# Linear attention outputs scaled head by head by ScalarE and turned by the identity; the third unit's first scores ahead of the first turns

## The reference, cut to what matters

```python
def gla_output(o, r, gain):
    B, T = o.shape[:2]
    o = o * lax.rsqrt(jnp.mean(o * o, axis=-1, keepdims=True) + EPS) * gain.astype(jnp.float32)
    return (o.reshape(B, T, GLA_V_W) * jax.nn.silu(r.astype(jnp.float32))).astype(r.dtype)
```

```python
def win_attend(qg, q_pos, k, v, k_pos, slopes):
    dist = (q_pos[:, None] - k_pos[None, :]).astype(jnp.float32)
    mask = (k_pos[None, :] >= 0) & (dist >= 0) & (dist <= WINDOW)
    s = jnp.einsum('bhgtd,bshd->bhgts', qg, k).astype(jnp.float32) * (NSA_HEAD_DIM ** -0.5) - slopes[None, :, :, None, None] * dist
    p = masked_softmax(s, mask)
    return jnp.einsum('bhgts,bshd->bhgtd', p.astype(v.dtype), v)
```

## Time and profile before

| | |
|---|---|
| median of 3 runs | 1752.52 us (1752.28 to 1753.33) |
| profiled execution, its own time | 1760.71 us |
| its span in the trace | 1758.9 us |
| TensorE matmuls busy | 1684.2 us, 96% of the span |
| VectorE busy | 1093.2 us, 62% |
| GpSimd busy | 830.2 us, 47% |
| ScalarE busy | 518.2 us, 29% |
| mean granted clock of TensorE | 0.978 of 2.4 GHz |
| linear attention stage | from 321.1 to 389.8 us of the span |
| sparse attention stage | from 390.0 us |

### The profile page before, as it was taken

One profiled execution on the slowest core, in us unless ns is written; L12 is line 12 of the kernel. 1 busy time (PEld: TensorE's weight loads), 2 busy tenths in 40 slices (PEclk: granted clock), 3 DMA queues, 4 the chain that ended last, 5 costly groups with the idle time before them and its releaser, 6 DMA issues.

```text
span 1758.9 us, 24643 instructions
## 1 busy us (share of the span) xinstructions
PE 1684.2 (96%) x9310; PEld 1369.3 (78%) x9310; DVE 1093.2 (62%) x2113; ACT 518.2 (29%) x1100; POOL 830.2 (47%) x644
## 2 busy tenths in 40 slices
PE   8999999897999989999999989999999999999997
PEld 7888888784555557777778878888888888888886
DVE  5332111446776667776641068896789678967897
ACT  3311111337887762334222162100120012001202
POOL 3211221314454452413222189957685668476933
PEclk9999999988999999999999999999999999999999
DMA  5488893838434545646643541121021201211005
GB/s 154 138 256 255 237 278 93 247 98 268 158 126 126 175 132 216 252 161 231 223 154 108 173 170 59 50 71 59 14 72 48 72 7 66 69 52 46 3 1 193
DMA packets 172396, 233.53 MB, mean 133 GB/s; under 512 B 22488, under 2 KB 137096, under 8 KB 168120
## 3 DMA queue, kind: packets, MB, share of 16 engines
q1 hardware_dynamic: 162024, 181.64, 33.6%
q0 software_dynamic: 9216, 50.34, 8.0%
q10 hardware_dynamic: 1040, 0.00, 0.0%
HBM read 217.58 MB, written 102.45 MB: 182 GB/s over the span
## 4 chain that ended last, share of the span: by engine, by line
PE 65%; DVE 6%; issue 2%; ACT 2%; POOL 2%; another core or an unknown queue 0%; DVEq 0%
PE PS L3137 36%; PE PS L2217 7%; PE PS L2415 6%; PE PS L1870 4%; PE PS L1855 4%; PE PS L1883 4%; DVE Z L2597 1%; DVE Z L3197 1%; POOL X L3071 1%; DVE Z L437 1%; PE PS L412 1%; POOL Z L1710 1%; PE PS L506 1%; PE PS L2261 0%; DVE Z L3157 0%
## 5 line engine op out<-in xcount | busy, mean ns | idle before, releaser
L3197 DVE TENSOR_TENSOR Z<-PS,Z 128x516 f32<-128x516 f32 x432 | 288.4, 686 | 118.8 <-PE PS L3137 117.5
L2217 PE MATMUL PS<-Z 128*128 128x256 f32 x768 | 189.4, 396 | 4.1 <-issue 3.2
L2217 PEld LDWEIGHTS PS<-Z 128*128 128x128 f32 x768 | 144.1, 196 | 33.4 <-issue 13.5
L3137 PE MATMUL PS<-Z,X 128*128 128x258 f32 x584 | 138.6, 384 | 2.6 <-POOL X L3071 2.6
L3137 PE MATMUL PS<-srow,misc 128*128 128x258 f32 x560 | 133.4, 381 | 0.0
L3137 PEld LDWEIGHTS PS<-Z,X 128*128 128x128 f32 x584 | 111.7, 192 | 19.9 <-POOL X L3071 3.0
L1144 DVE TENSOR_TENSOR Z<-PS,Z 128x516 f32<-128x516 f32 x27 | 18.8, 696 | 161.1 <-PE PS L312 161.1
L3137 PEld LDWEIGHTS PS<-srow,misc 128*128 128x128 f32 x560 | 106.0, 190 | 15.8
L3137 PE MATMUL PS<-srow,X 128*128 128x258 f32 x480 | 113.3, 380 | 0.0
L270 POOL TENSOR_TENSOR srow<-ring 128x512 f32<-128x512 f32 x15 | 21.2, 1410 | 194.0 <-PE PS L312 116.6
L3151 ACT ACTIVATE Z<-Z 128x2064 f32<-128x2064 f32 x16 | 30.8, 1924 | 248.2 <-DVE Z L3197 248.2
(11 more groups left out here) (484 smaller groups left out, 3827.7 us busy)
## 6 DMA issues: line engine op xcount, KB each, us to landing
packed_rows<-in_cache_nsa_kv SPq DMA_DIRECT2D x32, 1280.0 KB, 15.0
packed_blocks<-in_cache_nsa_kv SPq DMA_DIRECT2D x16, 2560.0 KB, 12.1
X<-in_w_ff_down SPq DMA_DIRECT2D x12, 1024.0 KB, 5.2
ring<-in_w_in SPq DMA_DIRECT2D x9, 1024.0 KB, 5.2
X<-in_x_prompt SPq DMA_DIRECT2D x8, 1024.0 KB, 13.1
ring<-in_w_ff_up SPq DMA_DIRECT2D x8, 1024.0 KB, 5.2
Z<-in_w_ff_up SPq DMA_DIRECT2D x8, 1024.0 KB, 5.2
out_y_prompt<-X SPq DMA_DIRECT2D x16, 512.0 KB
```

What stands on the lines that cost most here:

```text
L2217: last = nc.tensor.matmul(product(kind, v), w, x, start=(j == 0), stop=(j == 7))
L3137: last = nc.tensor.matmul(M.PS[:, N_.bank(n, e) + c, 0:HB], x[:, k, c * P:(c + 1) * P], y[:, k, :], start=e in (M1, M2, M5) and k == 0, st ...
L3197: nc.vector.tensor_tensor(N_.part(out, e), N_.view(n, e), N_.part(old, e), ALU.add).then_inc(N_.dve, 1)
```

## The change

`diagonals` goes away, and the buffer `dg` with it. ScalarE gets `scale_outputs(t)` in its place: four copies of 128x128, one for each head, in place in `Osb`, each with the factor of its token as scale. `turn_back` is then four transposes by the identity and no longer four products. In ScalarE's order `scale_outputs(t - 1)` stands behind `vk(t + 2)` and ahead of `out(t)`. GpSimd's tables are written without diagonals between them. In the sparse attention the scores of unit 2 that belong to the first piece of step 0 are put ahead of the turns of that piece.

```diff
@@ -1212,14 +1211,6 @@
-            def diagonals(t):
-                pool.wait_ge(rsr, t + 1)
-                if t >= 2:
-                    pool.wait_ge(ybk, t - 1)
-                pool.tensor_tensor(dg[:, t % 2], M.ident[:, :].rearrange("p (j n) -> p j n", j=1).to_broadcast([P, GH, P]),
-                                   root[:, t, :].rearrange("p (j n) -> p j n", n=1).to_broadcast([P, GH, P]), ALU.mult)\
-                    .then_inc(dgr, 1)
@@ -1252,12 +1243,9 @@
-            for t in range(QT):
-                diagonals(t)
-                if t in (1, 2, 3):
-                    templates(t - 1)
-                if t == 5:
-                    masks()
+            for i in range(3):
+                templates(i)
+            masks()
@@ -1330,13 +1318,13 @@
             def turn_back(t):
-                pe.wait_ge(dgr, t + 1)
+                pe.wait_ge(scd, t + 1)
                 pe.wait_ge(amr, min(t + 3, QT))
                 if t >= 1:
                     pe.wait_ge(fin, t)
                 for j in range(GH):
-                    last = nc.tensor.matmul(M.PS[:, X + j // 2, 256 + j % 2 * P:256 + (j % 2 + 1) * P], Osb[:, t % 2, j, :], dg[:, t % 2, j, :],
-                                            start=True, stop=True)
+                    last = nc.tensor.transpose(M.PS[:, X + j // 2, 256 + j % 2 * P:256 + (j % 2 + 1) * P],
+                                               Osb[:, t % 2, j, :], M.ident[:, :])
                 last.then_inc(ybk, 1)
@@ -1429,6 +1417,12 @@
+            def scale_outputs(t):
+                act.wait_ge(rsr, t + 1)
+                for j in range(GH):
+                    last = nc.scalar.activation(Osb[:, t % 2, j, :], Osb[:, t % 2, j, :], ACT.Copy, scale=root[:, t, j:j + 1])
+                last.then_inc(scd, 1)
+
@@ -1437,6 +1431,8 @@
                     scale(t - 1)
                 if t + 2 < QT:
                     vk(t + 2)
+                if t >= 1:
+                    scale_outputs(t - 1)
                 if t == QT - 1:
                     act.wait_ge(so, 1)
@@ -1446,6 +1442,7 @@
                 out(t)
             scale(QT - 1)
+            scale_outputs(QT - 1)
             act.wait_ge(so, 2)
@@ -1887,11 +1884,15 @@
             J = stages(n)
             for i in range(J):
+                opening = n == 0 and i == 0
+                if opening:
+                    for c in share(2 * nchunk[n + 2], i, J):
+                        score(n + 2, c)
                 for j in pair(n, i):
                     turn(n, j)
                 for j in pair(n, i - 1):
                     values(n, j)
-                if n + 2 < NSU:
+                if n + 2 < NSU and not opening:
                     for c in share(2 * nchunk[n + 2], i, J):
                         score(n + 2, c)
```

More of the change, by code:

```diff
@@ L1169, in phase_mid @@
     Osb = M.Zf[:, 23 * N:23 * N + 1024].rearrange("p (s j n) -> p s j n", s=2, j=GH)
-    dg = M.Zf[:, 22 * N:22 * N + 1024].rearrange("p (s j n) -> p s j n", s=2, j=GH)
     qs = M.misc[:, 2416:2432].rearrange("p (a b) -> p a b", a=2)
@@ L1182, in phase_mid @@
     orr, oev, sqr, ssr = T_("o_ready"), T_("o_moved"), T_("o_sq"), T_("o_ss")
-    rtr, rsr, dgr, ybk, fin = T_("o_root"), T_("o_scale"), T_("dg_ready"), T_("o_turned"), T_("o_mixed")
+    rtr, rsr, scd, ybk, fin = T_("o_root"), T_("o_scale"), T_("o_scaled"), T_("o_turned"), T_("o_mixed")
     stn, qsr, so, soe = T_("state_new"), T_("qs_ready"), T_("so_ready"), T_("so_moved")
```

## The result

Over 15 runs each the changed kernel took 1766.43 us (median; 1760.25 to 1779.82), the kernel before 1754.19 us (1752.28 to 1758.25). The ratio is 1.0084 (95% interval 1.0068 to 1.0101): 0.84% or some 14.7 us slower. The forecast was +10.4. The means, 1768.99 and 1754.40, are 14.6 us apart; the mean lies just beyond the range's upper end of 1768.6, and seven of the 15 runs lie above it. As a change the loss lies inside the range (+5.2 to +16.1 us, counted from the 1752.5 us of the first three runs of before). The profiled execution of after took 1774.51 us, 8 us more than its median, at a mean granted clock of 0.974; the fastest run had 0.983 and the slowest 0.971. The spread of 20 us (before: 6 us) goes with the clock.

A forecast was written before the change was run, and what follows sets the result against it. TensorE was taken to bound the linear attention, a chain through other engines the sparse attention's opening. Stage +8.6, clock +3.8, opening -2.0 make +10.4 us on 1752.5, rounded to 1762.5 us; range 1757.7 to 1768.6.

The forecast's parts named there:

- The mechanism: Linear attention: ScalarE's copies follow vk(t + 2), which waits for outputs(t), so turn_back waits for the formerly hidden scaling.
- Tiles 0 to 6: Linear attention steps: later turn_back adds 6.96 us over tiles 0 to 3; later sums add 1.17 over tiles 4 to 6.
- 8.6: Whole linear attention stage at unchanged clock, in us: 6.96 + 1.17 + 0.45, the last for tile 7.
- The clock, +3.8 us: Linear attention: new TensorE waits drop the clock to half in one of five steps, or parts of two; bounds 0 and 15.
- 8 to 13: Sign that the forecast is right: the linear attention stage, from 321 on, ends this many us later.
- The rival with the clock low in most steps: Linear attention: clock falls in three to four steps, +11 to +15 in place of +3.8; 1770 to 1774 us; chance 0.12.
- The opening: Sparse attention's start: four score products fill TensorE's 4.73 us idle time before the first turn; -2.0 us, bounds 3.4 and 0.
- The transposes: turn_back: four transposes take 0.66 us where eight product records took 1.16, 0.50 us less for each tile.
- scaling hidden: Linear attention: ScalarE scales tile t - 1 before outputs(t) ends, so -4.5 us, 1748.0 us; chance 0.05.
- GpSimd's freed work: Eight diagonals leaving GpSimd are worth nothing by themselves; its tables and masks are next needed in the sparse attention.

The follow-up runs named there:

- e4: The changed kernel with nine unused identity products in TensorE's wait ahead of turn_back, for tiles 0 to 4; ratio to before 1.0030.
- e6: The changed kernel with turn_back as float32 products by the identity in place of transposes; ratio to before 1.0089.
- e1: The kernel before with only the opening changed: unit 2's first scores ahead of the first turns; ratio 0.9986, 1757.54 against 1759.35 us.
- e2: The changed kernel with the opening put back as before, leaving ScalarE's scaling and the transposes; ratio to before 1.0091.
- e3: The changed kernel with scale_outputs(t - 1) ahead of vk(t + 2) in ScalarE's order; ratio to before 1.0003.
- e9: The kernel before with turn_back by transposes; diagonals still made and waited for but unused, outputs unscaled; ratio 1.0016.
- e5: The changed kernel without the four scaling copies, turn_back waiting for VectorE's reciprocal instead, outputs unscaled; ratio to before 1.0001.
- e13: The changed kernel with scaling ahead of vk and products by the identity for the transposes; ratio 0.9989, 1757.94 against 1759.96 us.
- e10: The kernel before with the opening alone, plus eight unused identity products among the second 32 of the 64 sample products; ratio 1.0032.
- e7: The changed kernel with turn_back behind scores and increments in TensorE's order, and its mask wait from t + 3 to t + 4; ratio to before 1.0136.

## Why the prediction was right or wrong

- **The mechanism: right.** Copies behind `vk`, `turn_back` behind the copies: six waits, 14.1 us, of which five and 11.5 us in the loop (the forecast was five or so and about 10). Four copies take 1.27 us (1.26 forecast), and each step has 2.2 to 2.4 us of idle time. The prediction wrote 2.4 for four steps and 1.7 for tile 0. The 1.7 is only what is added to the 0.62 us that TensorE waited there before; by its own rows the wait is 2.3 us, and it measured 2.21.
- **Tiles 0 to 6, +8.1 us at full clock: nearly right.** e4 shows it without the clock: sample products 7.1 us later than before, the whole stage 7.24 us longer and not 8.6; the step is 7.0 us and not 7.1.
- **The clock, +3.8 us: the step that failed.** "I expect the clock to fall in one of these five steps, or for parts of two." It fell at or right behind all five waits. Measured, e4 against after, it cost 9.5 us, two and a half times the term. It was the number of falls that was mis-sized and not the price of one: a step of 9.92 us at the clock of after against 7.0 in e4 is 2.9 us, less than the 3.8 taken. So the stage came out 22.85 us longer in the profile, where 8 to 13 had been named as the sign. The rival with the clock low in most steps (0.12) had the right mechanism, but at 1770 to 1774 it was above the medians. The forecast took a wait of 1.55 us over which the clock stayed and one of 2.73 over which it fell as a bracket, and put the new waits between them. One wait of each length doesn't make a bracket: in after the clock fell behind the very wait of 1.55 us, and in e6 it stayed over two of 2.43.
- **The opening, -2.0 us: right.** Alone it gives 2.5 us (e1). In after the first turn of step 1 comes 1.3 us earlier in the stage than before and not 2.9 as in e1; against e2, which lacks only the opening, it is 2.0.
- **The transposes, 0.50 us less per tile: right as a duration, wrong as a gain.** The four took 0.66 us. But VectorE's chain sets the start of the sample products, so 0.3 us arrives there (e3, e9), and the prediction took the 4.04 us of sample products as unchanged, where e3, e5 and e9 have 6.3 to 6.95. So the rival "scaling hidden", at 1748, would not have been reached even with its condition met: e3 meets it, and stands at 1.0003.
- **GpSimd's freed work at 0: nothing contradicts it.** e1, which keeps the diagonals, is no slower than e3 or e13, which don't have them.

With the measured sizes the sum is +7.2 (stage without the falls, e4) + 9.5 (clock) - 2.5 (opening, e1) = +14.2, against 14.7. The 9.5 is itself after less e4, so what this tests is e4 alone: +7.2 - 2.5 = +4.7 against the 5.3 measured. That the total of the forecast, +10.4, came within 4.3 us is partly luck: a step count too low by four was softened by too high a price for a step, and by what came back behind the stage in these profiles.

## What to carry to other kernels

When work moves from an engine that runs beside the critical one to one that waits for it, write down what stands ahead of it in that engine's order: here one call placed two lines higher was worth 14 us. Price a new wait of TensorE twice, as its length and as the work behind it at half clock. Don't read from one wait over which the clock stayed that waits of its length are safe, and give a low clock in most repeats as much weight as in one: it fell behind five of five in after and in e2, and behind three of five in e6. A shorter instruction on the bound engine pays only if the engine behind it is not the next limit; otherwise it buys idle time, and here that came with a lower clock.

## What was not expected of the hardware

- Waits of 2.2 us were enough: in after the granted clock went from 1.00 to 0.50 (2.4 to 1.2 GHz) with 2.21 us of idle time, and in e4, with the same waits filled, it stayed at 1.00 from 335 to 365. The length of the wait alone doesn't settle it: it stayed over 2.43 us in e6, and over 1.55 us in before but not in after.
- The 64 one-column float32 products took 3.84 us at full clock (e13) and 6.99 at half (after), 0.06 and 0.11 us each, and in every one of these profiles the clock was at half by the time they ended, or 0.1 us later (e6). Fillers among them didn't prevent it (e10). Whether it is these products or the idle times around them isn't shown.
- The times of after spread by 1.1% over its 15 runs and those of before by 0.3%; in after the slower runs have the lower mean clock (0.971 against 0.983 in the fastest). That idle gaps make the time less steady in general isn't shown: e6's six runs and e7's four, with gaps as long or longer, spread by 0.5% and 0.3%, and before spread by 0.4 to 0.5% in the later measurements.
